# A four-layer transformer kernel on one core: begun tiles taken two at a time, a reordered last attention pair, and a rebuilt opening

## The reference, cut to what matters

```python
def first_block(...):                 # layers 0 and 1
    for i in range(2):
        hn = rms_norm(h, g[0])
        y = mla_mixer(hn, ...) if i == 0 else dilated_mixer(hn, ...)
        h = h + rms_norm(y, g[1])
        h = h + rms_norm(swiglu(rms_norm(h, g[2]), ffn_w_in[i], ffn_w_out[i]), g[3])
        h = h + (p[i] @ ple_w_proj[i]) * sigmoid(h @ ple_w_gate[i])

def second_block(...):                # layers 2 and 3
    for l in range(2):
        x = layer_norm(ALPHA * x + hybrid_mixer(x, ...), ...)
        x = layer_norm(ALPHA * x + conv_ffn(x, ...), ...)

def mla_mixer(h, ...):                # the opening of the kernel
    a = h @ w_a                       # 1024 x 672
    c_q  = rms_norm(a[..., :384], q_norm)
    c_kv = rms_norm(a[..., 384:640], kv_norm)
    k_rot = apply_rope(a[..., 640:], positions)
    q = c_q @ w_uq;  kv = c_kv @ w_ukv    # 16 heads, then causal attention
```

## Time and profile before

| what | value |
| --- | --- |
| median of 3 runs | 1442.26 us (1441.75 to 1443.47) |
| the profiled execution, its own time | 1443.14 us |
| its span | 1441.3 us, so 1.8 us lie around it |
| PE, matmul busy | 1419.8 us (99%) |
| POOL / ACT / DVE busy | 1058.8 / 746.8 / 662.6 us |
| granted TensorE clock, mean | 0.999 |

### The profile page before, as it was taken

How to read it: one execution, slowest core, us unless ns; L and a number is a source line. 1 busy time by engine, 2 the same in 40 slices (tenths; PEclk the granted TensorE clock), 3 DMA queues, 4 the chain that set the end, 5 groups by cost and what they waited for, 6 DMA issues and landing times.

```text
span 1441.3 us, 21531 instructions
## 1 busy us (share of the span) xinstructions
PE 1419.8 (99%) x8654; PEld 1255.9 (87%) x8654; DVE 662.6 (46%) x1404; ACT 746.8 (52%) x997; POOL 1058.8 (73%) x262
## 2 busy tenths in 40 slices
PE   7999999999999999999999999999999999999997
PEld 6989888889899899798888889998888899998886
DVE  5646545034343333364540444666650566556614
ACT  6885545344666656565543445544543246344540
POOL 5376988865766666769888668759889677688891
PEclk9999999999999999999999999999999999999999
DMA  6576555555656556455555565355565555365560
GB/s 230 174 279 212 196 179 201 184 183 182 214 172 194 188 173 196 146 203 187 190 190 176 182 252 191 113 192 188 181 219 197 209 200 185 117 217 192 186 223 29
DMA packets 64667, 271.12 MB, mean 188 GB/s; under 512 B 6123, under 2 KB 28833, under 8 KB 37954
## 3 DMA queue, kind: packets, MB, share of 16 engines
q1 hardware_dynamic: 39704, 242.31, 49.3%
q10 hardware_dynamic: 24873, 27.53, 5.7%
HBM read 268.68 MB, written 8.21 MB: 192 GB/s over the span
## 4 chain that ended last, share of the span: by engine, by line
PE 94%; ACT 3%; DVE 2%; DMA 0%; issue 0%; SPq 0%; DVEq 0%; ACTq 0%
PE psum L464 90%; PE psum L656 1%; PE psum L942 1%; PE psum L542 0%; ACT w_hi L1130 0%; ACT prob L1362 0%; DMA h<-x 0%; PE psum L824 0%; PE psum L781 0%; PE psum L1088 0%; DVE xt_both L1703 0%; ACT q_rows L1329 0%; ACT prob L1446 0%; PE psum L1045 0%; ACT prob L1440 0%
## 5 line engine op out<-in xcount | busy, mean ns | idle before, releaser
L456 POOL TENSOR_TENSOR w_lo<-raw,w_hi 128x2048 fp32r<-128x2048 f32 (+2 forms) x248 | 1045.5, 4231 | 343.9 <-ACT w_hi L1130 343.9
L1130 ACT ACTIVATE w_hi<-raw 128x2048 fp32r<-128x2048 f32 (+2 forms) x248 | 432.1, 1753 | 139.5 <-DMA raw<-w_tail 87.3
L464 PE MATMUL psum<-xt_both,w_hi 128*128 128x512 f32 (+1 forms) x1920 | 442.7, 371 | 0.0
L464 PEld LDWEIGHTS psum<-xt_both,w_hi 128*128 128x128 f32 x1920 | 340.3, 189 | 57.1 <-issue 3.6
L464 PE MATMUL psum<-w_hi,xt_both 128*128 128x256 f32 (+3 forms) x1328 | 316.7, 328 | 0.5 <-DVE xt_both L1703 0.5
L464 PE MATMUL psum<-xt_both,w_lo 128*128 128x256 f32 x1728 | 253.5, 283 | 0.0
L464 PEld LDWEIGHTS psum<-w_hi,xt_both 128*128 128x128 f32 x1328 | 229.5, 190 | 15.4 <-issue 0.9
L464 PEld LDWEIGHTS psum<-xt_both,w_lo 128*128 128x128 f32 x1728 | 233.7, 191 | 7.5
L464 PE MATMUL psum<-w_lo,xt_both 128*128 128x256 f32 (+3 forms) x664 | 211.2, 326 | 0.0
L464 PEld LDWEIGHTS psum<-w_lo,xt_both 128*128 128x128 f32 x664 | 126.3, 190 | 7.1
L1218 ACT ACTIVATE lanes<-lanes 128x256 f32<-128x256 f32 x88 | 36.7, 418 | 166.5 <-DVE lanes L1740 107.8
(11 more groups left out here) (216 smaller groups left out, 1401.7 us busy)
## 6 DMA issues: line engine op xcount, KB each, us to landing
raw<-w_tail SPq DMA_DIRECT2D x156, 1024.0 KB, 4.9
raw<-w_dil SPq DMA_DIRECT2D x24, 1024.0 KB, 4.8
raw<-w_mix SPq DMA_DIRECT2D x24, 1024.0 KB, 4.9
raw<-w_dil SPq DMA_DIRECT2D x16, 576.0 KB, 3.7
bias_tiles<-bias_rows ACTq DMA_DIRECT2D x1, 6912.0 KB
gbuf<-gain_rows ACTq DMA_DIRECT2D x12, 512.0 KB, 5.0
dbias<-bias_tiles ACTq DMA_DIRECT2D x16, 384.0 KB, 5.8
raw<-w_dil SPq DMA_DIRECT2D x8, 384.0 KB, 4.6
```

The source lines that it names most:

```text
L456: nc.gpsimd.tensor_tensor(w_lo[:, s, 0:width], raw[:, s, 0:width], w_hi[:, s, 0:width].bitcast(F32), ALU.subtract).then_inc(lo_split, 1)
L464: return nc.tensor.matmul(dst, lhsT, rhs, start=start, stop=stop)
L1130: nc.scalar.activation(w_hi[:, s, 0:width], raw[:, s, 0:width], ACT.Copy).then_inc(hi_split, 1)
```

## The change

1. **Begun tiles in twos.** Two tiles share two chunks of 512 columns by half of the features each (`begun`), so a row product streams 512 columns into one bank instead of 256 twice. `TWOS` counts them: 2, 1, 2, 2, 2, so layers 0 and 1 begin 4 tiles, not 3.
2. **Turned back inside other products.** The first turn stands between the two halves of the next row product, the last between the halves of the first hidden tile.
3. **Last dilated pair.** DVE inverts head 0's sums behind its third maximum; ACT scales each head right after its exponentials, copies both turned heads in a row, and makes the two calls of `ahead` before and after all that.
4. **Opening.** `x` comes a second time as `xT`, by features, in four parts between the weight pieces, so PE's 16 transposes of `x` go. `a` is made without the outer root: ACT copies its rows for tb 0, DVE for tb 1. The outer root is made on DVE behind the angles, then the inner roots on GpSimd, with eps scaled. PE gets 12 products of zeros at the start. All bias copies come after the first heads, and small constants later.
5. **Preset.** Each `ffn` on ACT begins with a one-element activation of its function.

```diff
@@ PE, begin_tiles @@
+                def views_of(k):
+                    for half in range(2):
+                        if k == twos - 1 and half == 1:
+                            turn_block(t, 1)
+                        yield chunk(c + 2 * k + half, BANK)
...
-                for k in range(held):
-                    part(k, *views[k], 1)
-                    if k > 0:
-                        turn_back(k - 1)
-                then()
-                turn_back(held - 1)
...
+                for k in range(twos):
+                    part(k, [chunk(c + 2 * k + half, BANK) for half in range(2)], 1,
+                         (lambda: turn_back(k - 1)) if k > 0 else lambda: None)
+                then(lambda: turn_back(twos - 1))
@@ ACT, ffn @@
-                    if u + 2 < BEGUN[T_FFN[l]]:
-                        copy_rows(T_FFN[l], 1, [u + 2])
+                    if u == 0:
+                        copy_rows(T_FFN[l], 1, [1])
@@ POOL, inner_norms, called ahead of chunk C_MLA + 3 @@
+                pool.wait_ge(r0_ready, 1)
+                pool.wait_ge(squared, 2)
+                step(g.tensor_scalar(eps, var[:, 8:8 + TB], RMS_EPS, None, ALU.mult))
+                for k in range(2):
+                    ins = g.tensor_tensor(a[:, k * TB:(k + 1) * TB], eps, stat[:, k * TB:(k + 1) * TB], ALU.add)
+                step(ins)
+                g.tensor_scalar(half, a, -0.5, None, ALU.mult)
+                step(g.tensor_scalar(y.bitcast(I32), a.bitcast(I32), -0.5, 0x5F3759DF, ALU.mult, ALU.add))
+                for n in range(3):
+                    step(g.tensor_tensor(w, y, y, ALU.mult))
+                    step(g.tensor_tensor(w, w, half, ALU.mult))
+                    step(g.tensor_scalar(w, w, 1.5, None, ALU.add))
+                    ins = g.tensor_tensor(y, w, y, ALU.mult)
+                    if n < 2:
+                        step(ins)
+                ins.then_inc(ra_ready, 1)
@@ PE, the opening @@
+            def a_first(kt):
+
+                pe.wait_ge(x_lo_ready, kt + 1)
+                pe.wait_ge(piece_hi, kt + 1)
...
+                pe.wait_ge(piece_lo, kt + 1)
...
+            pe.wait_ge(warm_set, 1)
+            for _ in range(WARM):
+                mm(psum[:, 3, :], warm[:, 0:P], warm, True, True)
@@ ACT, the opening, behind the chunks of the first heads @@
+            act.wait_ge(a0_ready, 1)
+            nc.scalar.activation(a_rows[:, 0, :], flat[:, 0:MLA_A], ACT.Copy).then_inc(a0_copied, 1)
             act.wait_ge(ang_ready, 1)
             nc.scalar.activation(sin_p[:, :, :], ang[:, 0], ACT.Sin)
             nc.scalar.activation(cos_p[:, :, :], ang[:, 1], ACT.Sin).then_inc(sincos, 1)
...
+            act.wait_ge(a0_copied, 1)
+            a_squares(0)
+            act.wait_ge(a1_copied, 1)
+            a_squares(1)
             for tb in range(TB):
                 turn_hi_block(T_MLA_C, xt_hi, tb)
@@ DVE, behind the angles @@
+            e_r, r_r, half_r, w_r = [k[:, 8:8 + TB] for k in (var, rstd, nhalf, newton)]
+            dve.wait_ge(h_squared, TB)
+            step(v.tensor_scalar(e_r, stat[:, 2 * TB:3 * TB], RMS_EPS, None, ALU.add))
+            step(rsqrt_begin([(e_r, r_r, half_r, w_r)]))
             for n in range(3):
...
+                step(v.tensor_tensor(w_r, r_r, r_r, ALU.mult))
+                step(v.tensor_tensor(w_r, w_r, half_r, ALU.mult))
+                ins = v.scalar_tensor_tensor(r_r, w_r, 1.5, r_r, ALU.add, ALU.mult)
...
+            ins.then_inc(r0_ready, 1)
+
+            dve.wait_ge(chunk_used, 3)
+            v.tensor_copy(a_rows[:, 1, :], flat[:, 2 * BANK:2 * BANK + MLA_A]).then_inc(a1_copied, 1)
@@ ACT, the last dilated pair @@
             last = PAIRS - 1
+            ahead(C_WO[1])
             d_out(last - 1)
-            d_exp(last, 0)
-            ahead(C_WO[1])
-            d_exp(last, 1)
-            d_pscale(last, 0)
-            d_pscale(last, 1)
+            for hh in range(2):
+                d_exp(last, hh)
+                d_pscale(last, hh)
             d_pcopy(last, 0)
+            d_pcopy(last, 1)
             ahead(C_WO[1] + 1)
-            d_pcopy(last, 1)
             ahead(C_WO[1] + 1, LEAD)
```

More of the change, by code:

```diff
@@ L515, in begin_tiles, with part @@
             def begin_tiles(t, c, then):
-                held = BEGUN[t]
-                def part(k, hi, lo, tb):
+                twos = TWOS[t]
+                def part(k, views, tb, midway=lambda: None):
                     tok = slice(tb * P, (tb + 1) * P)
[L522 to L529, removed]
@@ L720, in ple @@
                 wide_block(1, 0, *proj, 1, ot, proj_at).then_inc(chunk_used, 1)
[L723 to L730, removed]
+            def a_first(kt):
+                pe.wait_ge(x_lo_ready, kt + 1)
+                pe.wait_ge(piece_hi, kt + 1)
+                c, at, n, _ = PIECES[kt]
+                cols, start, stop = slice(at, at + n), kt == 0, kt == KT - 1
+                hi, lo = w_hi[:, c, cols], w_lo[:, c, cols]
@@ L731, in a_product @@
                 for tb in range(TB):
                     tok = slice(tb * P, (tb + 1) * P)
-                    for j, kt in enumerate(kts):
-                        arrived(j)
-                        arrive(T_MLA, tb, kt)
-                        ins = split_x(psum[:, at[tb], 0:cols], xt_hi[:, kt, tok], xt_lo[:, kt, tok], hi[:, j, :], lo[:, j, :],
-                                      first and j == 0, last and j == len(kts) - 1)
-                    if tb == 0 and c == 2:
+                    mm(psum[:, 2 * tb, :], xt_hi[:, kt, tok], hi, start, False)
@@ L750, in bias @@
+            for kt in range(KT):
+                a_first(kt)
+            a_rest()
+            pe.wait_ge(ident_in, 16)
             def bias(g):
@@ L849, in _ @@
             mla_turn_first()
-            bias(2)
-            bias(3)
+            for g in range(2, NG + 1):
+                bias(g)
             mla_scores(0, True)
@@ L976, in d_step, with then @@
                 d_values_sum(pair, par)
[L978 to L979 removed]
+            def then(turn_last):
+                turn_r(2, T_DIL)
+                d_tiles(2, 0, turn_last)
+            begin_tiles(T_DIL, C_DIL, then)
             for n in range(3):
@@ L1962, in d_step @@
                             d_lo(pair - 1)
-                for hh in range(2):
-                    dve.wait_ge(d_exped, 4 * pair + 2 * hh + 2)
-                    v.reciprocal(rinv_q[:, :, hh:hh + 1], rsum_q[:, :, hh:hh + 1]).then_inc(d_inverted, 1)
+                        if col == 2 and not ahead:
+                            invert(0)
+                for hh in range(0 if ahead else 1, 2):
+                    invert(hh)
                 if ahead:
@@ L2145, in paired, with begun @@
             for j in range(n)]
+def begun(w, twos, n, left, right, step=P):
+    out = []
+    for j in range(0, 2 * twos, 2):
+        cols = np.concatenate([np.arange(at + u * step, at + u * step + P) for u in (j, j + 1) for at in (left, right)])
+        out += [tile(w, range(half * KT // 2, (half + 1) * KT // 2), cols) for half in range(2)]
+    return out + paired(w, n, left, right, step)[2 * twos:]
 def by_three(w, cols):
@@ L2174, in pack @@
         vcols = np.concatenate([np.arange(at(g, 2), at(g, 2) + P) for g in range(NG)])
-        steps.append([paired(wd, 1, at(g, 0), at(g, 1))[0] for g in range(NG)] + by_three(wd, vcols))
+        tiles = begun(wd, TWOS[T_DIL] if i == 0 else 0, NG, at(0, 0), at(0, 1), 3 * D)
+        steps.append(tiles + by_three(wd, vcols))
     out["w_dil"] = steps
@@ L2183, in pack @@
         out[f"w_mix{l}"] = [chunks]
-        rest = wide(a["w_out_2"][l - 2])[::-1] + paired(a["w_up_2"][l - 2], FT, 0, D_FF) + wide(a["w_down_2"][l - 2])
+        rest = wide(a["w_out_2"][l - 2])[::-1] + begun(a["w_up_2"][l - 2], TWOS[T_FFN[l]], FT, 0, D_FF) + wide(a["w_down_2"][l - 2])
         out[f"w_tail{l}"] = rounds(rest)
```

301 lines of the change are left out of this document (183 added, 118 removed).

## The result

The changed kernel takes 1450.48 us (1449.48 to 1451.12, 5 runs) against 1443.08 (1441.75 to 1444.79, 5 runs) for the kernel before on the same chip: ratio 1.0049, 95% interval 1.0038 to 1.0061. It is slower by 7.4 us. The prediction said 1437.9, range 1434.0 to 1440.8, and gave slower a chance of 0.05.

A forecast was written before the change was run, and what follows sets the result against it. It took PE, busy 99% of the span, as the bound, so time is matmuls times pitch. Gains of 3.3 (begun tiles), 0.2 (last dilated pair) and 0.9 (opening) sum to 4.4 us: median 1437.9, range 1434.0 to 1440.8.

The forecast's parts named there:

- `Preset`: a table load in a wait, nothing: One-element activation at each `ffn` on ACT: its table load falls in a wait, so no change in time.
- The opening: Start of the kernel up to the heads: earlier first products, partly lost to later bias copies, a gain of 0.9 us.
- PE starts at 30.4: Opening: PE's first product of the heads begins at 30.4 us instead of 32.13.
- the second rival: Opening gives nothing or costs: data for the heads come later behind `xT`; 2 us late gives 1439.9; chance 0.18.
- Three root steps were held beside three splits: Opening, outer root on DVE: one step gets through per POOL split, nine more after 26.0, done at 27.9 us.
- PE then runs as before: Opening, from PE's start to the first heads: unchanged pace, so 1.7 to 1.9 us earlier.
- the zero products: Opening, PE idle: taken as nothing; a half clock behind them outlasting 27 us would show the forecast wrong.
- POOL's fifteen steps: Inner roots on GpSimd: 0.3 us a step, 4.5 in all, done at 34.3; taken as nothing.
- The third rival: GpSimd's root steps become the bound at ACT's copy of q; at 1.3 us a step 1452.4; chance 0.05.
- The bias copies: Opening, ACT: two copies of 0.48 us each move from in front of the first heads to behind them.
- The begun tiles: Feed-forward tiles in twos: 4.4 us gained by wider products, 0.9 and 0.15 given back, 3.3 gained.
- The last dilated pair: Reordered scaling and copies: PE's sums start earlier, but `wo3`'s chunk comes later; 0.2 us gained, bounds 0 and 1.55.

The follow-up runs named there:

- a_inside: Changed kernel with `preset` laid into unused elements behind `stat`, so every tensor begins where it did in the kernel before: 1443.34 us, 0.9999 of the kernel before.
- b_shifted: Kernel before plus an unused five-element tensor ahead of `ht_hi`, moving what follows 32 bytes, no instruction changed: 1450.81 us, 1.0056 of the kernel before.
- a_zeros: Changed kernel with 16-element `preset` and products of zeros (6 and 16) in PE's two opening waits: 1447.84 us, against 1449.45 without the zeros.
- a_copy_first: Changed kernel with 16-element `preset` and DVE's copy of a's second rows ahead of its root steps: 1446.51 us, against 1449.45 without that move.
- b_begun: Kernel before with only the begun tiles in twos, turned back inside other products: 1440.90 us, 0.9984 of the kernel before.
- a_best: Changed kernel, no tensor displaced, DVE's copy ahead of its root steps, `wo3`'s chunk back between the last pair's copies: 1438.57 us, 0.9964 of the kernel before.
- a_line_copy: Changed kernel with 32-element `preset` and DVE's copy of a's second rows ahead of its root steps: 1445.81 us, 1.0020 of the kernel before.
- a_no_warm: Changed kernel with no tensor displaced and without the 12 opening products of zeros: 1444.08 us, 1.0007 of the kernel before.

## Why the prediction was wrong

**The step that failed most is a term put at nothing.** "`Preset`: a table load in a wait, nothing" priced the instruction and not the tensor. The tensor cost 7 us: by the pitches 7.0, by the medians 7.1 (the changed kernel less `a_inside`) and 7.9 (`b_shifted` less the kernel before, with a stretch of half clock in its profile). No rival had it, since all were about work and waits. That 1056 matmuls of a product which the diff doesn't mention could get longer was not asked.

**The opening: -0.9 predicted, +2.7 to +4.1 measured**, by the turn of the first probabilities in the four profiles with that opening (53.34 to 54.78). In its own steps:
- "PE starts at 30.4": 32.75. ACT, which waited for the heads' data, could copy them only from 21.16 and 22.90, where the sum had all of them by 20.05, so POOL split until 27.49 and not 26.0. That is the mechanism of the second rival. Three root steps were held beside three splits, as predicted. The root ended at 29.28, predicted 27.9, and the second bias product, which the change puts behind the second turn, stood between PE and the heads.
- "PE then runs as before": it ran at half clock. The text named a half clock only for the zero products. PE had stood idle twice, waiting for `a_rows`, and with both waits filled the clock stayed full (`a_zeros`). In the four profiles with this opening it fell at 24.9, 25.4, 27.1 and 29.0 us, twice between the waits and twice within the second. The prediction had no price for an idle stretch of PE.
- POOL's fifteen steps were right: 31.28 to 36.2, 0.33 each, 1.7 times DVE's 0.20. ACT found the roots ready since PE was later still. The third rival's mechanism appeared only once PE was mended (`a_copy_first`).
- The bias copies: 0.96 taken, and four of them stand in the chain at 0.35 and 0.48 as foreseen.

**The begun tiles: right.** 10.9 us for 48, 0.45 of waiting in layers 0 and 1 (`b_begun` and every later profile), none in layers 2 and 3, 3.2 in all by the profile and 3.0 to 3.5 by executions at equal clock. The plain median of `b_begun` shows 1.9 with an interval that holds 3.3.

**The last dilated pair: right in its parts.** By the timeline PE waited 1.07 before the second turn (1.2 predicted) and 1.30 for POOL before `wo3` (1.3 predicted), each 0.17 longer by the pitch; in all 0.2 lost and not 0.2 won. ACT's high part of that chunk began 0.34 later than in the sum: 24.22 us behind the start of PE's stretch of 96 matmuls (576.57 to 600.79), where the sum has 595.3 - 571.42 = 23.88. Of the bound of 1.55 some 1.0 was within reach: `a_best` takes 279.8 us from border to border where the kernel before takes 281.5, and 0.7 of that is in `b_begun` too.

**The size.** By the changed kernel's own profile 7.0 from the displacement, 5.0 in the opening (-0.9 to +4.1) and 0.4 in the last pair (-0.2 to +0.2): 12.4 of the 12.6 between 1437.9 and 1450.5.

## What to carry to other kernels

A tensor that is added to SBUF moves all that is allocated behind it, and with it the distance between operands of matmuls that nobody edited. Compare the pitch of every large group of matmuls before and after, not only of those in the diff, and put small new tensors into gaps or behind all others. Where executions differ in mean granted clock, compare those with the same one. And where PE waits for a few microseconds ahead of a stretch that is on the path, price that stretch at both clocks.

## What the hardware did that I had not expected

- The pitch of a split product with 512 streamed columns was 0.2267, 0.2324 or 0.2333 us, by the distance between streamed and stationary operand (0 or 256, 128, 32 or 64 bytes from the layout of before). With 256 columns a displacement of 64 bytes was a gain: 0.1178 and not 0.1199. The mechanism isn't known from these runs; beyond these only 192 bytes was tried, mixed with 128. The Trainium skill ("SBUF — State Buffer", who interferes with whom) has two independent read ports for PE, one for what streams and one for the weights. With both operands moved by 64 bytes the pitch stayed at 0.2267, with one moved it rose to 0.2333, so in this kernel the time still depends on where the two lie to each other.
- Waits of PE of 1.3 to 1.8 and 2.6 to 3.8 us in one opening were followed by a half clock in all four profiles with it, but from 24.9 to 29.0 us on and for 7 to 14 us; with a's copy first it fell in two profiles (`a_best`, `a_line_copy`) and not in the third (`a_copy_first`). The Trainium skill ("TensorE: Matmul & The Clock Gate", Part 1) says of the clock's rise that its moment varies from run to run; here the fall does. The spread of `a_no_warm` (1441.81 to 1445.68) goes with the clock: its four executions with a mean of 0.996 took up to 1443.26 us, the seven below that 1443.80 or more.
- Small dependent steps on GpSimd (operands of 2 to 4 elements) took about 0.3 us from start to start, the longest 0.45.
